# Yoco decoder trunk, first stage: where the norm weights are turned, who copies the turned memory rows, and when the second rows are squared

## The reference, cut to what matters

```python
def _rmsnorm(x, g):
    xf = x.astype(jnp.float32)
    y = xf * lax.rsqrt(jnp.mean(xf * xf, axis=-1, keepdims=True) + RMS_EPS)
    return (y * g.astype(jnp.float32)).astype(x.dtype)

def _mem_kv(mem, g, w_k, w_v):
    n, m, _ = mem.shape
    hm = _rmsnorm(mem, g)
    return ((hm @ w_k).reshape(n, m, MEM_HEADS, MEM_HEAD_DIM),
            (hm @ w_v).reshape(n, m, MEM_HEADS, MEM_HEAD_DIM))
...
mkv = [_mem_kv(mem_prompt, norm_mem_kv[l], mem_w_k[l], mem_w_v[l]) for l in range(DEPTH)]
```

## Time and profile before

| | us |
|---|---|
| median of 3 runs | 2330.92 |
| lowest and highest run | 2330.87, 2331.25 |
| the profiled execution | 2330.17 |
| its span (first to last instruction) | 2328.0 |

### The profile page before, as it was taken

One profiled execution on the slowest core, in us unless ns is written; L12 is line 12 of the kernel. 1 busy time (PEld: TensorE's weight loads), 2 busy tenths in 40 slices (PEclk: granted clock), 3 DMA queues, 4 the chain that ended last, 5 costly groups with the idle time before them and its releaser, 6 DMA issues.

```text
span 2328.0 us, 46539 instructions
## 1 busy us (share of the span) xinstructions
PE 2305.5 (99%) x19152; PEld 2277.1 (98%) x19152; DVE 1331.8 (57%) x1685; ACT 962.4 (41%) x1151; POOL 118.3 (5%) x142
## 2 busy tenths in 40 slices
PE   9999999999999999999999999999999999999998
PEld 8999998999999999999999998999999999999998
DVE  6778557555445554455656775675554455544554
ACT  7434455433333333333444434553333333333333
POOL 0000112000000000000111022110000000000001
PEclk9999999999999999999999999999999999999999
DMA  8665765555555555555566567645555555555553
GB/s 281 199 195 171 244 199 182 180 180 179 179 178 178 180 180 181 180 180 179 173 193 213 159 199 236 224 157 180 177 179 178 179 179 180 181 180 180 177 171 124
DMA packets 383561, 433.32 MB, mean 186 GB/s; under 512 B 14187, under 2 KB 350427, under 8 KB 382927
## 3 DMA queue, kind: packets, MB, share of 16 engines
q1 hardware_dynamic: 373902, 401.72, 54.0%
q0 software_dynamic: 8832, 29.49, 3.8%
q10 hardware_dynamic: 720, 0.58, 0.1%
HBM read 426.21 MB, written 6.45 MB: 186 GB/s over the span
## 4 chain that ended last, share of the span: by engine, by line
PE 98%; DVE 1%; ACT 0%; DMA 0%; issue 0%; DVEq 0%; SPq 0%; ACTq 0%
PE acc L798 30%; PE acc L800 30%; PE acc L799 30%; PE acc L875 1%; PE acc L876 1%; PE acc L883 1%; PE ab L1054 0%; DMA hA_flat<-in_mem_prompt 0%; PE acc L1009 0%; PE acc L978 0%; PE acc L988 0%; PE ab L894 0%; PE ab L978 0%; PE ab L945 0%; PE ab L1113 0%; PE ab L1091 0%
## 5 line engine op out<-in xcount | busy, mean ns | idle before, releaser
L798 PE MATMUL acc<-xs,whi 128*128 128x264 f32 (+1 forms) x3776 | 1081.0, 286 | 0.0
L800 PE MATMUL acc<-xs,wlo 128*128 128x264 f32 (+1 forms) x3776 | 1073.2, 284 | 0.0
L799 PE MATMUL acc<-xs,whi 128*128 128x264 f32 (+1 forms) x3776 | 1072.3, 284 | 0.0
L478 ACT ACTIVATE whi<-raw 128x1024 fp32r<-128x1024 f32 x744 | 762.4, 1054 | 713.8 <-DMA raw<-in_ffn_w_up 286.9
L1285 DVE TENSOR_TENSOR wlo<-raw,whi 128x1024 fp32r<-128x1024 f32 x744 | 876.8, 1230 | 200.6 <-ACT whi L478 176.6
L800 PEld LDWEIGHTS acc<-xs,wlo 128*128 128x128 f32 x3776 | 713.1, 189 | 0.0
L799 PEld LDWEIGHTS acc<-xs,whi 128*128 128x128 f32 x3776 | 710.7, 188 | 0.3
L798 PEld LDWEIGHTS acc<-xs,whi 128*128 128x128 f32 x3776 | 709.2, 188 | 0.3
L798 PE MATMUL acc<-hA,whi 128*128 128x264 f32 (+1 forms) x1216 | 346.3, 285 | 1.6 <-DVE hA L1569 1.6
L800 PE MATMUL acc<-hA,wlo 128*128 128x264 f32 (+1 forms) x1216 | 345.8, 284 | 0.0
L799 PE MATMUL acc<-hA,whi 128*128 128x264 f32 (+1 forms) x1216 | 345.0, 284 | 0.0
(11 more groups left out here) (293 smaller groups left out, 1131.8 us busy)
## 6 DMA issues: line engine op xcount, KB each, us to landing
raw<-in_ffn_w_gate SPq DMA_DIRECT2D x176, 512.0 KB, 3.4
raw<-in_ffn_w_up SPq DMA_DIRECT2D x176, 512.0 KB, 3.4
raw<-in_ffn_w_down SPq DMA_DIRECT2D x176, 512.0 KB, 3.6
raw<-in_dil_w_q SPq DMA_DIRECT2D x48, 512.0 KB, 3.6
raw<-in_pool_w_in SPq DMA_DIRECT2D x32, 512.0 KB, 3.6
raw<-in_pool_w_out SPq DMA_DIRECT2D x32, 512.0 KB, 3.7
raw<-in_mem_w_v SPq DMA_DIRECT2D x16, 512.0 KB, 7.1
raw<-in_mem_w_k SPq DMA_DIRECT2D x16, 512.0 KB, 6.6
```

What stands on the lines that cost most here:

```text
L478: nc.scalar.activation(half_block(whi, n, half), half_block(raw, n, half), ACT.Copy).then_inc(hi_ready, 1)
L798: mm(out, w_hi, hi_, start=first, stop=False)
L799: mm(out, w_hi, lo_, start=False, stop=False)
L800: return mm(out, w_lo, hi_, start=False, stop=last)
```

## The change

The norm weights lose their item `xload`; they are turned into `ab` ahead of the second rows, and ScalarE copies them out instead of VectorE. ScalarE also copies the second half of the first rows. The second rows are squared in two halves of 1024 columns, behind the high tiles 7 and 11, and the elementwise results of the squares go to `att` instead of `ab`. VectorE copies the last turned item behind tile 3 and the weight block there instead of ahead of all tiles, and makes the diagonals behind tile 11 instead of tile 1. The row statistics come behind the third block of `memv0` instead of the first. TensorE makes three products of ones into `ab` at three places between the turns. As `xload` is gone, the later items take the other pair of banks.

```diff
--- before.py
+++ after.py
@@ -53,7 +53,7 @@
 
 
 PHASES = [
-    ("memload0", 0, 2), ("memload1", 0, 1), ("xload", 0, 1), ("memload2", 0, 1),
+    ("memload0", 0, 2), ("memload1", 0, 1), ("memload2", 0, 1),
     ("memv0", 4, 1), ("memk0", 4, 2), ("memv1", 4, 1), ("memk1", 4, 2),
     ("win", 16, 8), ("grp", 4, 8), ("wout", 16, 8),
     ("mq0", 4, 2), ("mo0", 4, 8),
@@ -240,6 +240,7 @@
         h_ready = sem("h_ready")
         stat_ready, std_ready = sem("stat_ready"), sem("std_ready")
         ones_ready = sem("ones_ready")
+        gains_turned, gains_ready = sem("gains_turned"), sem("gains_ready")
         sq_ready, sq_added = sem("sq_ready"), sem("sq_added")
         xhi_ready, rows_summed, diag_ready = sem("xhi_ready"), sem("rows_summed"), sem("diag_ready")
         silu_ready = sem("silu_ready")
@@ -619,18 +620,19 @@
                     else:
                         at[0] = n + 4 * turns + 2
 
-            def rows_sum(key, c):
-
-                cached_landed(eng, key)
-                if c:
-                    eng.wait_ge(rows_summed, c)
-                nc.scalar.activation(ab[:, :, :].rearrange("p b c -> p (b c)"), cached(key), ACT.Square,
-                                     accum_out=ssqc[:, c:c + 1]).then_inc(rows_summed, 1)
+            def rows_sum(c, piece, pieces):
+
+                cached_landed(eng, ("mem", c))
+                if c + piece:
+                    eng.wait_ge(rows_summed, c + piece)
+                w, col = BLK // pieces, (0, 1, 4)[c + piece]
+                nc.scalar.activation(att[:, 0:w], cached(("mem", c))[:, w * piece:w * (piece + 1)], ACT.Square,
+                                     accum_out=ssqc[:, col:col + 1]).then_inc(rows_summed, 1)
 
             def x_rows_sum(c, half):
 
                 cached_landed(eng, ("x", c))
-                eng.wait_ge(rows_summed, 2 + 2 * c + half)
+                eng.wait_ge(rows_summed, 3 + 2 * c + half)
                 nc.scalar.activation(ab[:, 2:4, :].rearrange("p b c -> p (b c)"),
                                      cached(("x", c))[:, half * 1024:(half + 1) * 1024], ACT.Square,
                                      accum_out=ssqc[:, 2 + 2 * half + c:3 + 2 * half + c]).then_inc(rows_summed, 1)
@@ -647,24 +649,30 @@
                 eng.dma_start(gain_rows[16 * j:16 * (j + 1), P:2 * P], a[name].rearrange("(m p) -> m p", p=P)).then_inc(gains_in, 16)
             eng.dma_start(gain_rows[32:48, P:2 * P], a["pool_scale"].rearrange("l (m p) -> (l m) p", p=P)).then_inc(gains_in, 16)
             nc.scalar.preload_act_table(ACT.Copy)
-            eng.wait_ge(zeros_ready, 1)
-            for c in range(2):
-                rows_sum(("mem", c), c)
+            rows_sum(0, 0, 1)
+            eng.wait_ge(gains_turned, 1)
+            nc.scalar.copy(gains[:, :], ab[:, 0, 0:176]).then_inc(gains_ready, 1)
+            eng.wait_ge(turned, TURN0["memload0"] + 2)
+            copy_item(G0["memload0"] + 1, memT[:, 8:16, 0:P],
+                      acc[:, 2:4, :].rearrange("p b (s c) -> p (b s) c", c=P))
             at[0] = 1
             hi_half(0, 0)
-            eng.wait_ge(acc_free, G0["xload"] + 1)
+            eng.wait_ge(gains_ready, 1)
+            eng.wait_ge(acc_free, G0["memload1"] + 1)
             for m in range(DC):
                 if m == 8:
                     eng.wait_ge(acc_free, G0["memload2"] + 1)
                 high_x("memkv0", m, memT[:, m, :], TP)
                 if m == 1:
                     hi_half(0, 1)
+                if m in (7, 11):
+                    rows_sum(1, m // 4 - 1, 2)
                 if m % 4 == 3 and m < 12:
                     upto(1 + m // 4)
             eng.dma_start(mask[:, :, :], a["c_mask"]).then_inc(mask_in, 16)
             eng.dma_start(invc, a["c_inv"]).then_inc(mask_in, 16)
             root(STAT["mem"], TP)
-            eng.wait_ge(rows_summed, 2)
+            eng.wait_ge(diag_ready, 1)
             nc.scalar.activation(stdc[:, 0:2], ssqc[:, 0:2], ACT.Sqrt, bias=eps[:, :], scale=1.0 / D).then_inc(std_ready, 1)
             for m in range(DC):
                 c = GAIN["memkv"][1] + m
@@ -858,7 +866,7 @@
                         if m % 2 == 1:
                             last.then_inc(half_used, 1)
 
-            def value_phase(name, tile, ready, after=None):
+            def value_phase(name, tile, ready, after=None, after_block=0):
 
                 n, g = N0[name], G0[name]
                 item_free(g)
@@ -883,7 +891,7 @@
                             last = mm(acc[:, 2 * (g % 2) + c, :], x_hi, w_lo, start=False, stop=i == 3 and k == 3)
                         if k % 2 == 1:
                             last.then_inc(half_used, 1)
-                    if i == 0 and after is not None:
+                    if i == after_block and after is not None:
                         after()
 
             def side_turn(k, parts):
@@ -1157,12 +1165,20 @@
                 cached_landed(eng, ("mem", c))
                 turn_item(g, [(P, m, P, cached(("mem", c))[:, (8 * j + m) * P:(8 * j + m + 1) * P]) for m in range(8)])
 
+            def keep_busy(n):
+                for _ in range(n):
+                    mm(ab[:, 3, 0:P], ones[:, :], ones[:, :], start=True, stop=True)
+
             turn_memory(G0["memload0"], 0, 0)
             turn_memory(G0["memload0"] + 1, 0, 1)
+            eng.wait_ge(gains_in, GAINS_IN)
+            nc.tensor.transpose(ab[:, 0, 0:P], gain_rows[:, 0:P], ident[:, :])
+            nc.tensor.transpose(ab[:, 0, P:P + 48], gain_rows[0:48, P:2 * P], ident[0:48, 0:48]).then_inc(gains_turned, 1)
+            keep_busy(3)
             turn_memory(G0["memload1"], 1, 0)
-            eng.wait_ge(gains_in, GAINS_IN)
-            turn_item(G0["xload"], [(P, 0, P, gain_rows[:, 0:P]), (P, 1, 48, gain_rows[0:48, P:2 * P])])
+            keep_busy(3)
             turn_memory(G0["memload2"], 1, 1)
+            keep_busy(3)
 
             def turn_x(i):
                 c, j = divmod(i, 2)
@@ -1178,7 +1194,8 @@
                 side_turn(SIDE["st"] + j, [(P, m, TS * NST, cached(("state", 0), j)[0:TS * NST, m * P:(m + 1) * P])
                                            for m in range(8)])
 
-            value_phase("memv0", None, xs_wait("memkv0"), lambda: row_statistics(STAT["mem"], 1, False))
+            value_phase("memv0", None, xs_wait("memkv0"), lambda: row_statistics(STAT["mem"], 1, False),
+                        after_block=2)
             pair_item(N0["memk0"], G0["memk0"], 2, xtile, width=TP,
                       halves={0: lambda: turn_x_samples(), 1: lambda: turn_x(0), 2: lambda: turn_x(1), 3: lambda: turn_x(2)})
             pair_item(N0["memk0"] + 2, G0["memk0"] + 1, 2, xtile, width=TP,
@@ -1365,11 +1382,8 @@
                 v.tensor_copy(memT[:, 8 * j:8 * j + 8, c * P:(c + 1) * P], columns(g)).then_inc(acc_free, 1)
 
             memory_turned(G0["memload0"], 0, 0)
-            memory_turned(G0["memload0"] + 1, 0, 1)
+            eng.wait_ge(acc_free, G0["memload0"] + 2)
             memory_turned(G0["memload1"], 1, 0)
-            eng.wait_ge(turned, TURN0["xload"] + 1)
-            v.tensor_copy(gains[:, :], acc[:, 2 * (G0["xload"] % 2), 0:176]).then_inc(acc_free, 1)
-            memory_turned(G0["memload2"], 1, 1)
             eng.drain()
 
             def low_x(gen, m, src, width):
@@ -1388,10 +1402,12 @@
 
             def diagonals(c0):
 
-                eng.wait_ge(rows_summed, 6 if c0 else 2)
+                eng.wait_ge(rows_summed, 7 if c0 else 3)
                 if c0:
                     v.tensor_tensor(ssqc[:, 2:4], ssqc[:, 2:4], ssqc[:, 4:6], ALU.add)
-                    eng.drain()
+                else:
+                    v.tensor_tensor(ssqc[:, 1:2], ssqc[:, 1:2], ssqc[:, 4:5], ALU.add)
+                eng.drain()
                 for c in range(2):
                     last = v.tensor_scalar(sq_flat[:, c * P:(c + 1) * P], ident[:, :], ssqc[:, c0 + c:c0 + c + 1], None, ALU.mult)
                 return last
@@ -1434,10 +1450,13 @@
             eng.wait_ge(ident_in, 16)
             for m in range(DC):
                 low_x("memkv0", m, memT[:, m, :], TP)
-                if m == 1:
-                    diagonals(0).then_inc(diag_ready, 1)
                 if m % 4 == 3:
                     upto(m // 4)
+                if m == 3:
+                    memory_turned(G0["memload2"], 1, 1)
+                    eng.drain()
+                if m == 11:
+                    diagonals(0).then_inc(diag_ready, 1)
             rms(STAT["mem"], TP, 2)
             for m in range(6):
                 low_memory(m)
```

## The result

The changed kernel's median is **2336.89 us** (2335.23 to 2339.02); the kernel before, on the same chip, 2330.55 (2329.21 to 2332.74). The ratio is 1.0029, 95% interval 1.0020 to 1.0037: 6.3 us slower (4.7 to 8.6 by the interval), where 4.3 were forecast; the median lies 0.1 us above the upper end of the stated range.

What follows compares the result with a forecast made beforehand. TensorE's own work was taken as the bound, 98% of the chain; memk0 2.6 us later plus 1.7 us of slow clock made +4.3 on 2330.92, so 2335.2 us, range 2333.0 to 2336.8.

Steps and rivals of the forecast that it cites:

- steps 1 to 5: First stage: no gain at first product, clock held in block 0, later statistics, memk0 2.6 us later, slow clock 1.7 us.
- behind C: C is the end of VectorE's copy of the second rows, forecast at 13.85 us; block 1 starts at C + 7.45.
- the sum: Whole kernel: 2.6 us for the later memk0 plus 1.7 us of clock, +4.3 us.
- step 4: ScalarE's root waits for the row statistics ahead of memk0's weight halves: 3.8 us idle, memk0 2.6 us later, which stays.
- Step 5: At memk0: the 3.8 us idle stretch brings a slow clock stretch, price between 0 and 3.4 us, taken as 1.7.
- C's: Rival C: products of ones do not hold the clock in block 0, memk0 1.1 us later, 2336.3 us; 0.18 with twin.
- B: Rival: the clock holds through the new idle stretch ahead of memk0, costing only 2.6 us: 2333.5 us; chance 0.22.
- C's first half: In block 0: the products of ones do not hold the clock, and TensorE ends the block 1.7 us later, at 22.4.
- C's twin: A double slow clock stretch at memk0, 3.4 us, giving 2336.9 us; chance 0.18 together with C.
- D: Rival: the wait at ScalarE's root costs nothing because weight halves can be made before it: 2329.7 us; chance 0.06.

Runs made afterwards that it cites:

- the repaired order: Changed kernel with wide products of ones, memk0's first weight halves ahead of the root, sixteen highs later in two eights, VectorE likewise: 2329.50 us against 2329.99, ratio 0.9998.

## Why the prediction came out wrong, step by step

**What steps 1 to 5 say of the first stage was right.** Norm weights turned at 10.01 (10.35 forecast), second rows from 11.23 (11.5), first product 14.95 (15.1), block 1 at 21.00 released by VectorE's `xs` (21.3), statistics done at 32.6 (32.9), `memv0` done at 38.45 (38.5), idle 3.83 (3.8), `memk0` at 42.28 (42.3), slow stretch behind it 1.7 of lost clock (1.7). The small differences come from the transfers of the norm weights, which landed 0.3 us earlier. The cover for ScalarE's copies, 0.2 us in the prediction, was 0.6 (the copy ended at 11.78, VectorE's began at 12.38). Smaller slips: turning the weights took 0.45 us for the 0.35 set, three products of ones 0.77 for 0.66, and the terms of block 1 behind C add up to 7.52 and not 7.45. And two pieces cancel: the prediction set a product's start against the chain's 39.75 and so had 2.6 for the later `memk0`, which is 2.7 by starts, and the slow stretch cost 1.5 there and not 1.7. The first stage cost 4.2 us by products' starts, where the sum says 4.3. That the root is the cause, and not the copies or the squares in halves, is shown by the moved statistics alone (the same 3.8 us) and by the repaired order (none).

**What failed is the last sentence of step 4:** "Everything later is TensorE's own chain, so this stays." It was read from the shares of the chain, and nobody else does hold TensorE there. But TensorE also waits at one place of its own program, ahead of the 11,562nd product instruction, while a piece of program is loaded. The sum priced the nine products of ones (18 instructions) by their time at the start and by nothing behind it. In the nine traces with 19152 instructions the wait at L1113 or L1121 is none to 1.7 us, on average 0.9; in the nine with more it is 1.0 to 2.4, on average 1.8. In medians the number of instructions was worth 1.9 and 1.8 us in the one pair, and in the other 0.4 on one chip and 1.1 across two. The direction is the same each time. Against these stand the 1.8 and 1.55 us of work that 28 and 18 instructions push behind that place. But the kernel before had 0.7 in one trace and 1.7 in the other, so the number is not the only thing that sets this wait: in the first the load began while TensorE was at its 11,531st product instruction, in the second at its 11,560th. What makes the load begin late stays open.

**Step 5 took the clock for one stretch of one size.** In the traces of the changed kernel the granted clock lost 1.7 us at `memk0` twice and 3.4 once. Averaged over the three traces of the changed kernel and the two of before, the difference of 5.8 us (2334.0 against 2328.2) is made of 4.7 in the first stage (4.2, 5.65 and 4.0 against 0 and -0.1), 1.2 around L1121 (1.4, 3.0 and 0.7 against 0 and 1.1), and -0.1 at the end. The three comparisons of medians gave 6.3, 7.1 and 6.0. So of the 2 us that the sum lacks, about 1.2 are the program's loading (0.4 of it the slow stretch that came right behind the wait in one of the three traces), and 0.4 the uneven clock in the first stage. With three traces against two, whose late parts run from 0.7 to 3.0 and from 0 to 1.1, these shares are estimates. The rest, about half a microsecond, was not placed. The mean granted clock of the timed runs, 0.9981 for the changed kernel in all three sets and 0.9984 to 0.9986 for before, leaves room for it (0.0003 of 2330 us is 0.7), but part of such a loss, as in the last stage, costs nothing.

The range's upper end, 2336.8, was C's, and no case held a cost behind the first stage. The likeliest case, within 0.2%, was wrong with it; slower by over 0.2% had 0.39.

The rule cited in step 5 bears on this. The Trainium skill, TensorE: Matmul & The Clock Gate, Part 1 (What's actually happening), has the monitor run freely, so that the point of change shifts between runs; the traces agree, with a loss at 16 to 20 in one execution of before and at 11 to 19 in another. The sentence set against it, that three runs of before lie within 0.4 us, was weak: later runs of the same kernel span 2327.19 to 2331.63 on one chip and 2326.95 to 2333.75 on another.

**Rivals.** B (the clock holds) occurred in none of the seven traces with the idle stretch. C's first half is refuted: in block 0 the clock held in every trace of the changed kernel; in the second one the slow stretch fell on the turns ahead of it. C's twin, the double stretch at `memk0`, did occur, in that same trace. D is refuted as a forecast and true as a design: with the halves ahead of the root the first stage's loss is gone.

## What to carry to other kernels

Before moving a producer later, look at what stands *behind its consumer* on the consumer's in-order queue: here a root that nobody was in a hurry for stood ahead of weights that TensorE needed, and a cover of 2.8 us was spent by a move of 9.6 us. Filling idle time to keep TensorE's clock is worth it where the idling stands on the bounding engine, but with few wide products: here three of 512 columns won 2 us where fourteen of 128 won nothing. And where one engine fills 98% of the chain, its own instruction stream is still a resource with a price, to be looked for at waits that nobody releases.

## What the runs showed of the hardware that was not expected

- TensorE stopped at one place of its own program, ahead of the 11,562nd product instruction from the start, in 17 of 18 traces: for 0.3 to 2.4 us, ending 2.3 to 2.6 us behind the start of a 16 KB transfer on the instruction queue. It was longer on average (1.8 against 0.9) when 18 to 40 more instructions stood ahead, 1400 us earlier.
- In two traces such a wait (2.0 and 2.4 us) had a slow stretch right behind it, which cost another 1.3 us (0.6 in the shift, and 0.6 that before's own wait takes out of the shift there); in others with 1.7 to 2.1 us it had none.
- The last stage's turns took 3.6 us instead of 1.9 in an execution of the changed kernel and 3.3 in one of before, with a granted clock of 0.50 (the row above); in after little of it reached the end of the span. When the last writes landed the traces do not show.
- A product of ones with 48 columns took as long as one with 128 in the opening, 0.22 us for each instruction, while 128-column products of ones took 0.13 each at 10.5 us in after. The traces have no record of the clock in the opening (the first is at 6 us in before and after, at 15 in the kernel with 48 columns), so whether a slow clock is the reason stays open.
